# Two-head attention in a fused two-block kernel: VectorE divides the preceding item before it reads the scores of its own

## The reference, cut to what matters

```python
s = q @ k.T * scale + bias          # masked keys have a bias of -1e30 here
m = max(s)                          # window attention: also over a learned sink
p = exp(s - m)
p = p / sum(p)                      # window attention: sum(p) + exp(sink - m)
o = p @ v
```

## Time and profile before

| | us |
|---|---|
| three runs | 2193.67, 2185.86, 2192.00 |
| their median | 2192.0 |
| the profiled execution | 2189.02 |
| span of the profiled execution | 2187.2 |
| TensorE matmuls busy in it | 2147.8 (98%) |
| VectorE busy | 1011.3 (46%) |
| ScalarE busy | 851.4 (39%) |
| GpSimd busy | 893.5 (41%) |

### The profile page before, as it was taken

The page is one execution under the profiler, slowest core; times in us unless marked ns, Lnnn a source line. Parts: engine busy times, 40 slices in busy tenths (PEclk is TensorE's granted clock), DMA queues, the critical chain, the costliest instruction groups (busy, mean ns, idle before and its releaser), DMA issues.

```text
span 2187.2 us, 27277 instructions
## 1 busy us (share of the span) xinstructions
PE 2147.8 (98%) x10205; PEld 1724.7 (79%) x10205; DVE 1011.3 (46%) x1491; ACT 851.4 (39%) x1282; POOL 893.5 (41%) x684
## 2 busy tenths in 40 slices
PE   9999999999999999999999999999999999999999
PEld 7775787788888867766888888888888877888887
DVE  5755646586626152475432231346634755323121
ACT  6435645432222243565432232444433334423221
POOL 5421255154444443212444444433433325444443
PEclk9999999999999999999999999999999999999999
DMA  4212132133322342101222222322222213222222
GB/s 168 75 67 77 49 101 83 49 101 121 106 99 98 111 129 73 49 30 56 92 99 98 99 97 97 105 85 70 76 87 77 78 39 108 98 98 98 98 97 96
DMA packets 55109, 193.23 MB, mean 88 GB/s; under 512 B 6112, under 2 KB 6368, under 8 KB 54752
## 3 DMA queue, kind: packets, MB, share of 16 engines
q1 hardware_dynamic: 50112, 180.41, 24.8%
q10 hardware_dynamic: 4896, 11.41, 1.6%
HBM read 189.69 MB, written 2.10 MB: 88 GB/s over the span
## 4 chain that ended last, share of the span: by engine, by line
issue 53%; POOL 29%; PE 17%; POOLq 1%; ACT 0%; DMA 0%; DVE 0%; SPq 0%; ACTq 0%
POOL wl L552 29%; PE gemm_ps L587 6%; PE gemm_ps L588 6%; PE gemm_ps L589 6%; POOLq L549 0%; POOLq L561 0%; ACT xh L1836 0%; DMA x<-x_in 0%; ACT wh L1441 0%; PE turn_ps L708 0%; DVE x L2150 0%; SPq L526 0%; ACTq L1835 0%
## 5 line engine op out<-in xcount | busy, mean ns | idle before, releaser
L552 POOL TENSOR_TENSOR wl<-raw,wh 128x512 fp32r<-128x512 f32 x678 | 889.8, 1335 | 1275.8 <-ACT wh L1441 1275.8
L1441 ACT ACTIVATE wh<-raw 128x1024 fp32r<-128x1024 f32 x339 | 358.7, 1059 | 751.4 <-DMA raw<-w_in 740.0
L587 PE MATMUL gemm_ps<-xh,wh 128*128 128x512 f32 x1192 | 471.7, 396 | 0.9 <-DVE arena L2037 0.9
L589 PE MATMUL gemm_ps<-xh,wl 128*128 128x512 f32 x1192 | 464.5, 390 | 0.0
L588 PE MATMUL gemm_ps<-xl,wh 128*128 128x512 f32 x1192 | 464.3, 390 | 0.0
L588 PE MATMUL gemm_ps<-arena_r,wh 128*128 128x512 f32 (+1 forms) x1088 | 416.9, 383 | 0.0
L587 PE MATMUL gemm_ps<-arena_r,wh 128*128 128x512 f32 (+1 forms) x832 | 319.9, 385 | 1.2 <-POOL wl L552 0.8
L589 PE MATMUL gemm_ps<-arena_r,wl 128*128 128x512 f32 (+1 forms) x832 | 317.3, 381 | 0.0
L587 PEld LDWEIGHTS gemm_ps<-xh,wh 128*128 128x128 f32 x1192 | 224.0, 188 | 51.2 <-issue 3.9
L588 PEld LDWEIGHTS gemm_ps<-xl,wh 128*128 128x128 f32 x1192 | 224.1, 188 | 48.2 <-issue 2.4
L589 PEld LDWEIGHTS gemm_ps<-xh,wl 128*128 128x128 f32 x1192 | 223.9, 188 | 47.0
(11 more groups left out here) (410 smaller groups left out, 2521.4 us busy)
## 6 DMA issues: line engine op xcount, KB each, us to landing
raw<-w_in SPq DMA_DIRECT2D x338, 512.0 KB, 3.4
arena<-na_in ACTq DMA_DIRECT2D x14, 256.0 KB, 2.7
out<-x ACTq DMA_DIRECT2D x8, 256.0 KB, 2.9
x<-x_in SPq DMA_DIRECT2D x6, 256.0 KB, 6.5
arena<-alibi_in ACTq DMA_DIRECT2D x6, 256.0 KB, 3.7
arena<-moba_in ACTq DMA_DIRECT2D x1, 1024.0 KB, 4.8
arena<-mem_in ACTq DMA_DIRECT2D x1, 1024.0 KB, 4.8
arena<-dist_in ACTq DMA_DIRECT2D x1, 896.0 KB, 4.9
```

The source lines that it names most:

```text
L552: m = pool.tensor_tensor(wl[:, k, half], raw[:, k, half], wh[:, k, half].bitcast(F32), ALU.subtract)
L587: pe.matmul(o, wh[:, n % RING, w], h[:, kt, 0:width], start=(kt == 0), stop=False)
L589: last = pe.matmul(o, wl[:, n % RING, w], h[:, kt, 0:width], start=False, stop=(kt == nkt - 1))
L1441: act.activation(wh[:, k % RING, :], raw[:, k % RING, :], ACT.Copy).then_inc(high_split, 1)
```

## The change

On VectorE, in `pair_attention`, the division of the preceding item moves ahead of the reading of the step's own scores. The function is shared by all three lists. The attention to the memory, `cross_attention`, has an order of its own, which stays.

```diff
                 n = len(items)
                 for i in range(n + 4):
+                    if 1 <= i <= n:
+                        divide(i - 1, items[i - 1])
                     if i < n:
                         logits(i, items[i])
-                    if 1 <= i <= n:
-                        divide(i - 1, items[i - 1])
                     if i >= 4 and items[i - 4]["last"]:
                         outputs(items[i - 4])
                     between(i)
```

## The result

| | before | after |
|---|---|---|
| median of 6 runs, us | 2189.48 | 2200.03 |
| lowest and highest | 2185.86 to 2193.67 | 2196.05 to 2201.63 |
| profiled execution | 2189.02 | 2201.03 |
| its span | 2187.2 | 2199.2 |
| its mean granted clock | 0.995 | 0.992 |

The ratio of the times is 1.0046, 95% interval 1.0028 to 1.0063: 10.5 us slower. (Three of the six runs of before are the ones shown ahead of the prediction.) By that interval the kernel is slower by 6 to 14 us: the sign is clear, the size is not.

The account below looks back on a forecast made before the run. TensorE work fills most of the program; in the third stage TensorE waits 6.1 us for VectorE's read of scores. Terms 6.4 + 2.1 + 1.1 + 1.4 = +11.0 us on a median of 2192.0 give 2203.0; range 2197 to 2208.

Parts of the forecast that it names:

- The third stage, +6.4: Third list (16 items, 953 to 1013 us): a closed loop of read, exponentials and divide costs +6.4 us, bounds 5 to 8.
- The loop's two terms: Third stage: 15 turns of read, exponentials and divide, 45.1 us; extras on top, splits 4.5 and group outputs 3.8.
- The second stage, +2.1 + 1.1: Second list (16 items, 852 to 953 us): +2.1 from later reads from step 9 on, +1.1 from GpSimd's pair in step 10.
- The 0.7 that it saw at step 12: Second stage, step 12: a divide of 0.94 behind the group output, of which 0.7 us shows.
- between nothing and 2.1: Second stage, step 10: cost in us of item 9's divide meeting GpSimd's pair with the read behind it; half taken, +1.1.
- The first stage, +1.4: First list (8 items, 205 to 262 us): +0.9 in step 7 and about 0.5 in step 6; bounds 0.9 and 1.6.
- the term of 0.9: First stage, step 7: later read, then ScalarE's exponentials, whose queue TensorE waits for at 261.00; +0.9 us.
- The 0.5 for GpSimd in step 6: First stage, step 6: the divide falls into GpSimd's pair (247.22 to 249.75), adding about 0.5 us.
- rival D: TensorE's clock falls in longer idle times; given nothing beyond C, no chance of its own.
- A, no loss: All stages: the divide fits VectorE's idle time ahead of the read at every step; 2192, at best 2190; chance 0.10.
- B, part cover: Some third-stage turns are shorter as ScalarE shifts or TensorE's pieces cover more; +5 to +8, 2197 to 2200; chance 0.15.
- C, collisions at every meeting: GpSimd's pair falls more than once on divides that hold up reads, each up to 2.1; +14 to +16; chance 0.12.

Follow-up runs that it names:

- wait_only: Kernel before, with only the wait for the preceding item's exponentials moved ahead of the read, the divide left behind it; 2189.5 us, ratio 1.0003.
- double_before_read: Changed kernel, with each item's probabilities multiplied by 1.0 once more just before the divide, ahead of the read; 2222.2 us, ratio 1.0152.
- ahead_deferred: Changed kernel, with the third list's group outputs and row-block splits moved behind the next read; 2193.9 us, ratio 1.0024.
- window_only: Kernel before, with the divide ahead of the read in the second list alone (16 items with the sink); 2191.5 us, ratio 1.0018.
- moba_only: Kernel before, with the divide ahead of the read in the first list alone (8 items); 2191.8 us, ratio 1.0014.
- neighbour_only: Kernel before, with the divide ahead of the read in the third list alone; 2192.7 us, ratio 1.0026.
- deferred: Kernel before, read still ahead of divide, with the third list's group outputs and row-block splits moved behind the next read; 2186.4 us, ratio 0.9989.

## Why the prediction was right where it was, and what failed

**The third stage, +6.4, was right in size and cause.** 46.1 became 52.4, +6.3, at a clock of 1.00 throughout, with the turns of 2.93 and 3.27 in place of 2.95 and 3.30 and 53.3 for all of them in place of 53.4. The signs named came out: L2210 waits for L1551, L2200 no more for L832, the wait of scores grew from 6.1 to 15.0 ("over 12"), the stretch lasts 67 ("66"), and transposes wait for L2213 no more. The loop's two terms were tested apart: the divide's time ahead of the read (wait_only, double_before_read) and the extras (ahead_deferred).

**The second stage, +2.1 + 1.1, was right in its size and in the two steps that carry most of it.** scores(10) came 0.5 later and scores(11) 2.5, where the text had 0.45, and 1.4 in all with 1.1 on top for GpSimd. The 0.7 that it saw at step 12 came a step later, at scores(14). The meeting was where it was put, in the divide of item 9: 1.75 in place of 0.75, so +1.0 of "between nothing and 2.1". The Trainium skill (SBUF — State Buffer, section "SBUF: two separate sides") has the later starter blocked for the whole of the other's instruction; that VectorE's second division was held for about one of GpSimd's two instructions agrees. In the profile of window_only the stage is +3.4 against 3.2. It has a fall of the clock too, 0.79 from 928 to 936 us, but one that cost little: from scores(11) to scores(12) it is 5.57 where before had 5.39, the slower matmuls filling the 1.20 that TensorE had waited there for the divide. In the change's profile the stage is +4.9, with 0.57 in those 8 us: the 1.5 more lie behind the wait of 2.47, in slower matmuls.

**The first stage, +1.4, was mis-sized by its term for GpSimd.** ScalarE's copy came later and TensorE waited 3.56 in place of 2.26 at L851, so the term of 0.9 has its row: the wait's end is 261.58, 0.58 later on the clock of a stage that began 0.44 earlier, which is 1.0; moba_only against window_only and wait_only has 0.9. The 0.5 for GpSimd in step 6 is on VectorE's timeline (at 248.57 two divisions take 1.15 in place of 0.62) but didn't reach the total: TensorE's work there covered it. The rest of the profile's +2.6 is the clock, 0.79 from 260 to 268 us where before had 1.00. At equal clock moba_only is +0.5.

**The term wrongly put at nothing was rival D, "I give it nothing beyond C".** I took the clock for unmoved because the 2.26 us of idle time at 261 had cost none in that one execution. In the change's profile it fell at 263 and at 928, which cost 1.6 and 1.5 us; in double_before_read, with longer waits still, all four runs have 0.987 or 0.988. The mean clock of before is 0.9941 over 78 runs and that of the change 0.9925 over 6. How much of the total that is, is not settled. At 1.84 us per 0.001 it is 2.9 us and leaves 8.3 for the loop and the two steps, 2.7 less than my 11.0. By the profiles the three lists are 0.9, 3.4 and 6.3, together 10.6, and with a mean of the change's runs 11.2 over the mean of before that leaves 0.6 for the clock.

**The profiles are the better witness, I think, because the line takes off too much.** neighbour_only's third stage had a mean clock of 0.937 over 54.1 us, which the line prices at 2.9; it was 1.7 longer than the change's own at full clock. In window_only the fall behind scores(11) cost about 0.2, and the line prices it at 1.4. Together that is 2.4 taken off too much in these two. For the averages it is not shown, as only one run of each kernel was profiled. The whole-kernel median of +10.5 lies near my +11.0; with an interval of some 4 us either way, that it lies so near is luck.

**The level** was off by another 2.5 us. I added 11.0 to a median of three runs, 2192.0; that of six was 2189.5, that of 78 was 2187.7. The profiled execution, 2189.0, was the better base.

**The rivals.** A, no loss, fell: each of the three stages grew. It was true of the wait and false of the divide. B, part cover, has the third stage at 5.0, which is what the totals give at equal clock; the change's profile, with 6.3 at full clock, speaks against it. C, collisions at every meeting, fell: of the two meetings with a divide ahead of a read that after shows (248.57 and 925.81), only the second held up a read for which TensorE waited. The pair of the third stage started at 978.02 after, 0.05 behind the end of a divide (977.35 + 0.62), and met none; in the kernel before, at 968.05, it had lengthened two divisions by 2.1.

## What to carry to other kernels

In a queue worked in order, what another engine waits for goes ahead of what only has to be done some time; ask it of every operation, the small extras too: here they were worth more (3.8 us, gained in deferred) than the wait that wait_only moves ahead of the read (0.2). Price such a move as a closed loop, release to release, and compare the turn with what the other engine needs in a turn: where the loop is shorter it costs nothing. And where an effect is below 1%, put each run's granted clock beside its time before believing a median, and don't believe the correction either until a profile shows what a fall cost.

## What the hardware showed that I had not expected

TensorE's granted clock fell not only behind idle time. In window_only it was 0.57 on average from 216 to 224 us with matmuls busy 8.00 of 8.00, and the same code ran at 1.00 in before. TensorE's timeline, window_only:

```profile
216.00 2.39 PE L657 MATMUL gemm_ps<-con,y_all 128*128 128x2 f32 x16
218.26 0.77 PE L587 MATMUL gemm_ps<-xh,wh 128*128 128x512 f32 x1
218.83 0.63 PE L588 MATMUL gemm_ps<-xl,wh 128*128 128x512 f32 x1
...
223.95 0.40 PE L588 MATMUL gemm_ps<-xl,wh 128*128 128x512 f32 x1
```

The matmuls start 0.43 apart up to 223.5 and 0.23 after, which are the two levels of 1.2 and 2.4 GHz. Around the fall's start stand sixteen matmuls of 2 columns each. The falls at 928 and 263 in the changed kernel stand by waits of 2.47 and 3.56. But the wait of 2.26 at 261 in before has no fall behind it, and the same wait of the same code in window_only (2.25, ending at 264.44) has one, the 0.81 from 260 to 268 us shown above. So a single profile does not tell what a wait costs in clock, and I had taken one for a rule. What decides which execution gets a fall is open.

The Trainium skill (TensorE: Matmul & The Clock Gate, section "Part 1: The HAM clock gate") says that a monitor sets the clock by how busy the engine has been, that it runs free of the kernel's start and so differs from run to run, and that for a model the ramp at a kernel's start is under 1% of a typical span. The runs agree that it differs from run to run of the same code; what the monitor looks at, no run here shows. All that the clock takes in before is of that size too: 0.991 to 0.996 is 0.4% to 0.9% lost. But from run to run that is 0.5% of the clock and 10 us of the time, and the effect sought was 0.5%; and in double_before_read the loss was 1.3%.

How long GpSimd's pair delayed a divide went with the moment at which they met. At 968.06 before, the two divisions took 2.69 in place of 0.62; one by one they took 1.41 and 1.36, each about as long as the instruction of the pair beside it (1.28 and 1.32). At 925.81 after, it was 1.75 in place of 0.75: the first took 0.42 and the second 1.42, about one instruction of the pair. The difference that the rows show is that the first met the pair at its start (968.06 against 968.05) and the second 0.18 ahead of it (925.81 against 925.99), so that one division was already under way. At 248.57 after, the divide met the second instruction of a pair half done: the first division took 0.89, up to about that instruction's end at 249.31, and the second 0.34 as usual.
